# Expert value products with the value columns stationary and the token weights moving

## The reference

```
q      = h @ w_q                                   # 8 heads, two key halves
s1, s2 = scores against 128 + 128 sub-keys, the 16 best of each, then the 16 best of 256 sums
gates  = softmax(top)                              # 8 * 16 = 128 experts for each token
act    = gelu(einsum('td,ted->te', h, u[expert]))
out    = einsum('te,ted->td', gates * act, v[expert])     # 256 x 1024
x      = x + g2 * out
```

## Time and profile before

| | us |
|---|---|
| median of 3 runs | 3439.9 (3437.94 to 3444.47) |
| profiled execution, its own time | 3442.56 |
| profiled execution, span from first to last instruction | 3440.7 |
| TensorE busy in the span | 3354.9 (98%) |
| VectorE busy | 2458.5 (71%) |
| ScalarE busy | 1631.8 (47%) |

### The profile page before, as it was taken

One profiled execution on the slowest core, in us unless ns is written; L12 is line 12 of the kernel. 1 busy time (PEld: TensorE's weight loads), 2 busy tenths in 40 slices (PEclk: granted clock), 3 DMA queues, 4 the chain that ended last, 5 costly groups with the idle time before them and its releaser, 6 DMA issues.

```text
span 3440.7 us, 69595 instructions
## 1 busy us (share of the span) xinstructions
PE 3354.9 (98%) x24630; PEld 3023.9 (88%) x24630; DVE 2458.5 (71%) x5105; ACT 1631.8 (47%) x3275; POOL 362.7 (11%) x480
## 2 busy tenths in 40 slices
PE   8999999999999999999999999999999999999998
PEld 7878889988888998889888888888889888888887
DVE  6744457765434867447998888888439998888887
ACT  5253356433434743145555555555446555555554
POOL 0212000020210010000460000000000640000000
PEclk9999999999999999899999999999999999999999
DMA  8733379874335985134348778888345258888885
GB/s 230 180 86 94 107 228 273 243 190 133 84 94 171 276 249 143 51 108 147 94 114 198 195 194 194 194 197 193 101 124 168 77 141 194 193 196 195 195 195 134
DMA packets 644021, 565.18 MB, mean 164 GB/s; under 512 B 62027, under 2 KB 589402, under 8 KB 643546
## 3 DMA queue, kind: packets, MB, share of 16 engines
q1 hardware_dynamic: 638564, 542.16, 60.6%
q0 software_dynamic: 4960, 19.93, 1.7%
q10 hardware_dynamic: 278, 0.08, 0.0%
HBM read 550.52 MB, written 9.44 MB: 163 GB/s over the span
## 4 chain that ended last, share of the span: by engine, by line
PE 82%; DVE 13%; ACT 2%; issue 1%; DMA 1%; POOL 0%; SPq 0%; DVEq 0%; ACTq 0%; POOLq 0%
PE bank L1478 15%; PE bank L883 14%; PE bank L861 14%; PE bank L1495 7%; PE bank L1498 7%; PE bank L1492 7%; PE bank L904 4%; PE bank L1453 2%; PE bank L857 2%; DVE uT L3366 2%; PE bank L1287 1%; DVE arena L3289 1%; DVE arena L3280 1%; PE bank L984 1%; DVE arena L3281 1%
## 5 line engine op out<-in xcount | busy, mean ns | idle before, releaser
L1478 PE MATMUL bank<-t_high,u_parts 128*128 128x256 f32 x3072 | 420.7, 279 | 1.3 <-ACT u_parts L2217 1.3
L1478 PEld LDWEIGHTS bank<-t_high,u_parts 128*128 128x128 f32 x3072 | 398.5, 188 | 20.4 <-ACT u_parts L2217 2.9
L3405 DVE TENSOR_TENSOR v_low<-ring,v_high 128x512 fp32r<-128x512 f32 x512 | 336.8, 689 | 59.3 <-ACT v_high L2229 35.2
L1495 PE MATMUL bank<-v_high,w_low 128*128 128x512 f32 x1024 | 322.3, 396 | 0.0
L1498 PE MATMUL bank<-v_low,w_high 128*128 128x512 f32 x1024 | 321.8, 395 | 0.0
L1492 PE MATMUL bank<-v_high,w_high 128*128 128x512 f32 x1024 | 320.9, 394 | 0.9 <-ACT v_high L2229 0.9
L2229 ACT ACTIVATE v_high<-ring 128x512 fp32r<-128x512 f32 x512 | 298.2, 618 | 38.2 <-PE bank L1498 38.2
L2217 ACT ACTIVATE u_parts<-bank 128x512 fp32r<-128x512 f32 x384 | 220.2, 596 | 191.7 <-DVE bank L3377 188.6
L1781 ACT ACTIVATE arena<-bank 128x256 f32<-128x256 f32 (+1 forms) x270 | 104.1, 388 | 416.5 <-PE bank L861 233.3
L861 PE MATMUL bank<-hT,ring 128*128 128x256 f32 (+2 forms) x1232 | 279.2, 383 | 6.6 <-DVE hT L2675 6.1
L861 PE MATMUL bank<-arena,ring 128*128 128x256 f32 (+2 forms) x1168 | 270.8, 386 | 5.8 <-DVE arena L3111 3.0
(11 more groups left out here) (477 smaller groups left out, 6375.0 us busy)
## 6 DMA issues: line engine op xcount, KB each, us to landing
ring<-in_peer_v SPq DMA_DIRECT2D x256, 512.0 KB, 4.6
ring<-in_peer_u SPq DMA_DIRECT2D x768, 128.0 KB, 4.3
ring<-in_w_in SPq DMA_DIRECT2D x128, 512.0 KB, 4.0
ring<-in_mlp_up SPq DMA_DIRECT2D x64, 512.0 KB, 4.5
uT<-in_mod_w SPq DMA_DIRECT2D x64, 512.0 KB, 5.2
ring<-in_mlp_down SPq DMA_DIRECT2D x64, 512.0 KB, 4.9
ring<-in_peer_u SPq DMA_DIRECT2D x64, 512.0 KB, 3.9
arena<-in_mod_w POOLq DMA_DIRECT2D x32, 512.0 KB, 5.0
```

The source lines that it names most:

```text
L1478: ins = eng.matmul(PB[6 + b][:, 0:S], u_parts[:, part, k * P:k * P + P], moving[:, k, :], start=(n == 0), stop=(n == len(products) - 1))
L1495: eng.matmul(PB[2 * tt + q][:, :], w_low[:, b, t], v_high[:, d], start=False, stop=False)
L3405: tt_(v_low[:, j % 4, d], ring[:, 2 + j % 4, d], v_high[:, d].bitcast(F32), ALU.subtract).then_inc(sem("vL_ready"), 1)
```

## The change

The roles in `combine` are exchanged. A chunk `c` of 128 value columns is stationary, and the 256 token weights move. `expert_sum(c)` gives each of the eight chunks half a bank: chunks 0 and 1 in bank 0, to 6 and 7 in bank 3. A half `q` of the values now has three products of four matmuls each with 256 moving columns, in place of three of two with 512. The result has the value columns on its partitions, as `xT` has. The copies to `moe_t`, the transposes and their semaphores go, and VectorE's 8 steps read banks 0 to 3 directly, the first four when the last tile's first half is done, the others when its second is.

Since these banks now hold the sums until VectorE has read them, the first tiles of the next layer's projection (`raw_bank`, labels that begin with "c") go to banks 5 to 7, and the sums of squares go to bank 4. `mod` is allocated ahead of `tab` and `wT`, which moves these two by 96 words. A semaphore of the output is renamed.

```diff
@@ SBUF tensors
+        mod = sb("mod", [P, DEPTH, MOD])
         tab = sb("tab", [P, 2, 2, S])
         wT = sb("wT", [P, 2, S])
-        mod = sb("mod", [P, DEPTH, MOD])
@@ helpers
+        def raw_bank(label):
+            t = tiles[label][0]
+            return PB[(5 if label[0] == "c" else 0) + t % BANKS]
+        def expert_sum(c):
+            return PB[c // 2][:, (c % 2) * S:(c % 2) * S + S]
@@ TensorE, combine
-                    tokens = [slice(tt * P, tt * P + P) for tt in range(TT)]
                     for q in range(2):
-                        d = slice(q * 512, q * 512 + 512)
+                        chunks = [(c, slice(c * P, c * P + P)) for c in range(4 * q, 4 * q + 4)]
                         eng.wait_ge(sem("wH_ready"), i * 8 + (j + 1 + base))
                         eng.wait_ge(sem("vH_ready"), i * 16 + (2 * j + q + 1 + 2 * base))
-                        for tt, t in enumerate(tokens):
-                            eng.matmul(PB[2 * tt + q][:, :], w_high[:, b, t], v_high[:, d], start=first, stop=False)
+                        for c, d in chunks:
+                            eng.matmul(expert_sum(c), v_high[:, d], w_high[:, b, :], start=first and c % 2 == 0, stop=False,
+                                       skip_group_check=True)
                         eng.wait_ge(sem("wL_ready"), i * 8 + (j + 1 + base))
-                        for tt, t in enumerate(tokens):
-                            eng.matmul(PB[2 * tt + q][:, :], w_low[:, b, t], v_high[:, d], start=False, stop=False)
+                        for c, d in chunks:
+                            eng.matmul(expert_sum(c), v_high[:, d], w_low[:, b, :], start=False, stop=False, skip_group_check=True)
                         eng.wait_ge(sem("vL_ready"), i * 16 + (2 * j + q + 1 + 2 * base))
-                        for tt, t in enumerate(tokens):
-                            ins = eng.matmul(PB[2 * tt + q][:, :], w_high[:, b, t], v_low[:, j % 4, d], start=False, stop=last)
+                        for c, d in chunks:
+                            ins = eng.matmul(expert_sum(c), v_low[:, j % 4, d], w_high[:, b, :], start=False,
+                                             stop=last and c % 2 == 1, skip_group_check=True)
                         ins.then_inc(sem("v_free"), 1)
@@ TensorE, behind the loop
-                for k in range(KD):
-                    if k % 4 == 0:
-                        eng.wait_ge(sem("experts0_ev"), pe.next("experts0_ev"))
-                        eng.wait_ge(sem("experts1_ev"), pe.next("experts1_ev"))
-                    for tt in range(TT):
-                        ins = eng.transpose(PB[4 + k // 2][:, (k % 2) * S + tt * P:(k % 2) * S + tt * P + P],
-                                            moe_t[:, tt, k * P:k * P + P], C("ident"))
-                    if k % 2:
-                        ins.then_inc(sem("moe_mm"), 1)
@@ ScalarE, behind the loop
-                eng.wait_ge(sem("v_free"), 2 * (base + NKEY))
-                for q in range(2):
-                    eng.activation(moe_t[:, 0, q * 512:q * 512 + 512], PB[q][:, :], ACT.Copy).then_inc(sem("experts0_ev"), 1)
@@ VectorE, behind the loop
-                eng.wait_ge(sem("v_free"), 2 * (base + NKEY))
-                for q in range(2):
-                    eng.tensor_copy(moe_t[:, 1, q * 512:q * 512 + 512], PB[2 + q][:, :]).then_inc(sem("experts1_ev"), 1)
                 if l == 0:
                     gains(1, 0, raw_c)
                 for k in range(KD):
-                    if k % 2 == 0:
-                        eng.wait_ge(sem("moe_mm"), dve.next("moe_mm"))
-                    stt_(xT[:, k, :], PB[4 + k // 2][:, (k % 2) * S:(k % 2) * S + S], mod[:, l, 40 + k:41 + k],
+                    if k % 4 == 0:
+                        eng.wait_ge(sem("v_free"), 2 * (base + NKEY) - 1 + k // 4)
+                    stt_(xT[:, k, :], expert_sum(k), mod[:, l, 40 + k:41 + k],
                          xT[:, k, :], ALU.mult, ALU.add).then_inc(sem("x_ready"), 1)
```

More of the change, by code:

```diff
@@ L608, in two_stacks @@
         one_p = uT[:, 1, :].rearrange("p (b t e) -> p b t e", b=2, t=4)
-        moe_t = area(0, TT, D)
         out_t = area(0, TT, D)
@@ L1001, in raw_columns @@
                         tile_ready("raw_ready", base + k + 1)
-                        ins = eng.matmul(PB[t % BANKS][:, 0:S + 1], wv[:, k, :], raw[:, k, :], start=(k == 0), stop=(k == KD - 1))
+                        ins = eng.matmul(raw_bank(label)[:, 0:S + 1], wv[:, k, :], raw[:, k, :], start=(k == 0), stop=(k == KD - 1))
                     ins.then_inc(sem("unit_done"), 1)
@@ L1715, in _ @@
                 else:
-                    raw_columns([("c", j) for j in range(RAW)], raw_c, 3)
+                    raw_columns([("c", j) for j in range(RAW)], raw_c, 4)
                     for j in range(RAW, 6):
@@ L1748, in _ @@
                 expert_tiles(l)
-            norm_sum(0)
+            norm_sum()
             norms[0] += 1
@@ L2619, in _ @@
                 eng.wait_ge(sem("out_ready"), q + 1)
-                eng.wait_ge(sem("experts1_ev"), 2 * DEPTH + q + 1)
+                eng.wait_ge(sem("out_copied"), q + 1)
                 eng.dma_start(out[0].rearrange("(a p) d -> p a d", p=P)[:, :, d], out_t[:, :, d]).then_inc(sem("stored"), 16)
@@ L2693, in raw_out @@
                 t = tiles[label][0]
-                ps, col = PB[t % BANKS], small[:, 44:45]
+                ps, col = raw_bank(label), small[:, 44:45]
                 eng.wait_ge(sem("unit_done"), last_unit(label))
@@ L3510, in _ @@
                 else:
-                    inv_norm(D, 1e-6, 3)
+                    inv_norm(D, 1e-6)
                     raw_out(("c", 0), lat[:, 0, :])
@@ L3545, in _ @@
                 expert_tiles(l)
-            norm(hT, vec[:, 3, VEC3["final_norm_2"][0]:VEC3["final_norm_2"][0] + 8], eps=1e-6, bank=0)
+            norm(hT, vec[:, 3, VEC3["final_norm_2"][0]:VEC3["final_norm_2"][0] + 8], eps=1e-6)
             for q in range(2):
                 eng.wait_ge(sem("out_mm"), dve.next("out_mm"))
-                eng.tensor_copy(out_t[:, 1, q * 512:q * 512 + 512], PB[2 + q][:, :]).then_inc(sem("experts1_ev"), 1)
+                eng.tensor_copy(out_t[:, 1, q * 512:q * 512 + 512], PB[2 + q][:, :]).then_inc(sem("out_copied"), 1)
 def kernel(**inputs):
```

## The result

The changed kernel takes 3450.9 us (median of 18 runs, 3444.2 to 3460.3), the kernel before 3442.6 us (18 runs beside them, 3436.7 to 3450.2). The ratio is 1.0023, with a 95% interval of 1.0015 to 1.0030: 8.3 us slower. That is rival 2, which was priced at 3449 against 3439.9, or 9.1 us slower, and given 0.22.

What follows compares the result with a forecast made beforehand. TensorE's matmul pace was taken to bound the kernel. From the profiled 3442.6 us, one loop of each pace (-8.0) and the ends (-5.3) gave 3429.3, against the median 3426.6, said as 3427; range 3402 to 3450.

Steps and rivals of the forecast that it cites:

- rival 2: Both layers' expert loops locked at the slow matmul pace, 117.4 ns: slower than before, 3449 us, chance 0.22.
- What bounds the kernel: Expert loops: TensorE's matmul count times pace sets the time; a change of pace passes to the end one to one.
- The prices of the cases: Expert loops: both fast 30.4 us less, both slow 14.4 us more, one of each 8 us less.
- all three cases: Whole kernel: both loops fast 3404 us (chance 0.25), one of each 3427 (0.46), both slow 3449 (0.22).
- A stretch therefore enters a pace and keeps it: 256-column matmuls in the loops: a whole stretch holds one pace, 113.4 or 117.4 ns each.
- I give each pace one half: Each layer's loop enters its pace for itself, fast or slow with equal chance.
- I take 0: Loop waits for rounded weights and values: no added cost; 13 us if the cover were gone.
- Rival 3: A wait appears at successive value products, +13 us, about 3440; one of four rivals sharing chance 0.07.
- Where the operands lie: Moving `mod` shifts the weights by 96 words, changing the distance between matmul operands; costed at 0.
- Nothing of 512 columns parts them any more: Scores in the loops: join the products' stretch at its pace, where before they alternated, 2.785 us in the mean.
- Behind the loops: Between each loop's end and the norm: earlier steps onto `xT` save 2.7 and 2.6 us, 5.3 in sum.
- Rival 4: Value products alone go slow, scores stay as they are: 7.7 us more in the loops, 3442 us, chance 0.03.

Runs made afterwards that it cites:

- e5: Changed kernel, two late VectorE transposes woven into its waits for ScalarE: median 3438.1 us, in groups 3399.0 to 3405.9, 3425.6 to 3428.1, 3448.1 to 3460.6.
- e1: Changed kernel with `mod` back in its old place, value products' operands 48 and 52 words apart: 3452.3 us, ratio 1.0029 to the kernel before.
- e3: Changed kernel with the weights' tensors 64 words further on, value products' operands 16 and 20 words apart: 3451.9 us, ratio 1.0029 to the kernel before.
- e8: The changed kernel run once more as it is: 3451.7 us, ratio 1.0024 to the kernel before.
- e2: The kernel before with only the allocation of `mod` moved as in the change: 3439.8 us, ratio 0.9989.
- e13: Kernel of e5 plus one extra 384-column matmul in each layer, in the first pass: 3404.8 us, ratio 0.9888 to the kernel before.
- e4: Changed kernel with VectorE's two late transposes moved whole behind their tile's other work: 3476.9 us, ratio 1.0101 to the kernel before.
- e6: Changed kernel plus an extra 64-column matmul ahead of each of 14 passes a layer: 3441.7 us, ratio 0.9994 to the kernel before.
- e11: Kernel of e5 plus an extra 128-column matmul ahead of each of 14 passes a layer: 3429.3 us, ratio 0.9957 to the kernel before.
- e14: Changed kernel, transposes not woven, plus an extra 384-column matmul in each of 14 passes a layer: 3424.1 us, ratio 0.9935 to the kernel before.
- e7: Changed kernel plus an extra 512-column matmul ahead of each of 14 passes a layer: 3442.7 us, ratio 0.9999 to the kernel before.
- e10: Kernel of e5 plus an extra 512-column matmul ahead of each of 14 passes a layer: 3432.3 us, ratio 0.9967 to the kernel before.
- e12: Kernel of e5 plus an extra 384-column matmul ahead of each of 14 passes a layer: 3408.9 us, ratio 0.9905 to the kernel before.

## Why the prediction was wrong

- **What bounds the kernel**: right. TensorE has no idle time worth the name in the loops, and the change of its pace went on to the end (13.6 us in the loops).
- **The prices of the cases**: right. Both slow was 3449 against 3439.9, +9.1, and +8.3 was measured. The three groups of e5 answer to all three cases, and a slow loop cost 7.9 us where 14.4 / 2 = 7.2 was said.
- **"A stretch therefore enters a pace and keeps it"**: the step that failed, with what stands on it, "I give each pace one half". Only the slow pace is kept. The fast one outruns the chain of VectorE and ScalarE, a pass of 38.07 us of matmuls gets through in 38.37, and one of its stalls sooner or later leaves the pace slow (two fast loops of the profiles ended so after two passes). Nor was the entry even: behind the wait at the loop's beginning 3 of 14 loops began fast. With e5's reordering, which removes both waits, 9 of 24 loops in its 12 runs were fast by the times, with single paces kept to the end. What the rival of both loops slow said, that a loop which starts slow never leaves the slow pace, held for five of the eight profiled loops; its price was right, its chance of 0.22 too low. None of the 44 runs of the changed kernel, e1, e3 and e8 was below 3444 us, where an even draw would put three of four.
- **"I take 0" for the waits**: right for the direct cost (1.4 us of idle before the 2048 matmuls of the first row, where 0.9 was), wrong in what it left out. I compared 0.04 us a half with a margin of 0.34 as if each half started afresh. The lateness sums over the half pass in which VectorE never waits for TensorE, to some 0.72 us; the measured shift is 0.60. And I asked only what a wait would cost, not what it would do to the pace. Rival 3 had a wait "mostly on a slow or mixed loop", at +13 us; it comes on the fast pace in each pass, and on the slow one once in e8.
- **Where the operands lie**: costed at 0, and for the new form e1 and e3 confirm it within 0.1%; the likeliest suspect of the change was innocent. For the old form it isn't nothing: in e2 the move alone changed products and scores, by amounts that nearly cancel.
- **"Nothing of 512 columns parts them any more"** as the reason why the scores alternated: not shown, and e2 speaks against it as it stands, since there the same products stand between 84 slow scores on end.
- **Behind the loops**: 5.3 us less was forecast from the starts of the norm; 2.80 and 2.74 us came out there, 5.0 us in the account. This is read in the profiles; no run tested it alone.
- **Rival 4** (the scores stay as they are): excluded, the scores of the second layer are all slow. The Trainium skill (TensorE: Matmul & The Clock Gate, Back-to-back issue gap) states 262 cycles for 256 columns, by which an estimate is 109 ns, and gives it for the isolated gap of a single matmul. The traces agree at neither pace, 113.3 or 117.6 ns, and the sign that its rule gives came out for another reason: at the fast pace the same matmuls gain 30 us.
- The sign of what the edit itself allows is thus the other way round. The change makes a fast loop possible (31 us less in the two loops of e13) and at the same time puts an end to the alternation in which every second score was fast. Which of the two counts depends on short waits for the work of another engine.

What stays open: why a stretch enters one pace and not the other, how much of the slow loops is due to the wait at their beginning and how much to the later stalls, why 384 columns left it fast each time while 128 and 512 turn it over (but for one case) and 64 go slow, slow, fast, why the scores of the kernel before alternate and those of e2 don't, and what the 4 ns are. The regular orders of e4 and e6 say that more than chance is at work. The mechanism between widths and pace is a rule found in single profiles. e4 and e11 to e14 rest on 4 timed runs each.

## What to carry to other kernels

Where one engine sets the time, count its instructions per window in several places, before and after: a mean length on the page (279 to 281 ns here) hides that the same matmul has two prices, and an edit that removes another form of instruction can change which of them holds. A margin is to be compared with the gain summed over all steps between two points at which the other engine waits for the bounding one, here half a pass, and not with one step's gain. And a result between two states calls for the run times one by one: e5's median says "nothing", its twelve times say that some 50 us lie between its outer groups (means 3402.0 and 3452.8).

## What was unexpected of the hardware

- Back-to-back 128x256 fp32r matmuls, each with a weight load of its own, run at 113.3 or 117.6 ns apiece at one granted clock (1.00), and keep either for over 5000 matmuls (e5).
- A single matmul of 512 columns turned the pace over 56 times of 56 (e7, e10), one of 128 columns 27 times of 28 (e11); one of 384 columns, whose slot was 2819.15 - 2818.97 = 0.18 us long, left it fast 58 times of 58, seven of them from slow (e12 to e14); one of 64 turned fast into slow 8 times of 8 and slow into fast 11 times of 20 (e6). A stall of TensorE of 0.1 to 0.9 us may turn it or not (e4, e8, e14).
- Distances of 16, 48 and 80 words between the operands' starts make no difference over 0.1% for 256 columns (e1, e3). With 512 columns a move of the weights by 96 words took the products from 233.0 to 230.1 ns a matmul and ended the alternation of the 256-column scores beside them (e2).
